# Key searches of four blocks moved from the attention stage into the projection stage, with attention of those blocks first and the weights' upper parts rounded on GpSimd

## The chip, the cores and the metric

The kernel runs on one core of one Trainium2 chip. The metric is the device time of one execution in microseconds (us), the median of three runs.

## The reference

The program computes two layers over one sequence of 2048 positions and width 1024. The change touches the first layer. There, after a root-mean-square norm, one matrix product gives the inputs of two branches. One is a recurrence over the positions (eight heads of 64). The other is sparse attention: each position scores all earlier keys with a small index network, keeps the best 256, and attends to those alone.

```python
def attend(args):                       # one block of 128 queries
    qa, qi, wi, t0 = args
    causal = key_pos[None, :] <= (t0 + jnp.arange(Q_BLOCK))[:, None]
    logits = jnp.einsum('bqhd,bsd->bqhs', qi, k_idx)        # 4 index heads
    score = jnp.einsum('bqh,bqhs->bqs', wi, jax.nn.relu(logits))
    score = jnp.where(causal[None], score, -jnp.inf)
    _, idx = lax.top_k(score, topk)                         # topk = 256
    c_sel = jax.vmap(lambda c, i: c[i])(c_kv, idx)
    s = jnp.einsum('bqhr,bqkr->bhqk', qa, c_sel)            # 8 heads
    s = jnp.where(valid[:, None], s, -jnp.inf)
    return jnp.einsum('bhqk,bqkr->bqhr', jax.nn.softmax(s, axis=-1), c_sel)
```

Both branches are gated, joined, multiplied by an output matrix and added to the input. The second layer is latent attention with rotary positions and a small memory attention; the change leaves it alone.

## The kernel before

**Stages.** The program is a row of stages, each with one function per engine (`pe_a`, `act_a`, `dve_a`, `pool_a` and `sp_a` for the projection stage, the same with `_2` for the attention stage). Between two stages every engine drains and waits for all others.

**Projection stage.** The sequence is taken in four chunks of 512 positions, in two halves of two chunks. The input product has 25 weight tiles of 1024x128. Each is read from memory into `raw_a` (two buffers), rounded to its upper part `wah` (piece `("w", s)`, on ScalarE in `act_a`), and the rest is left in `wal` (VectorE). Both have four buffers. A product of a tile with a chunk (piece `p`) is 24 matmuls: upper by upper, upper by lower and lower by upper, for eight slices. Its results go to one of three PSUM banks and are copied out by ScalarE or VectorE. Beside the products run pieces for the norms and queries (`sum`, `mean`, `qq`), and, for each pair of heads and 256 positions, a chain that makes the operands of the recurrence (`dd`, `lora`, `decay`, `kk`, `vt`, `bk`, `bt`, `bonus`); there are 32 such steps, 16 in each half. `kk` holds a square root, whose table in ScalarE is another than that of exponential and hyperbolic tangent. Input rows are turned and split into `xc` by the pieces `in` and `tr`; the last of them is done soon after the second half has begun, and leaves `xin`, `xtmp` and `xjunk` unused from then on.

**Attention stage.** 16 blocks of 128 queries, the longest first: block `b` has `128 * (nth(b) + 1)` keys, with `nth(b) = 15 - b`. For blocks with more than 256 keys the key search comes first. Piece `log`: matmuls of the index queries with 512 keys, relu on ScalarE, weighted sum on VectorE into `score`, mask on GpSimd. Then the value of the 256th best score is found bit by bit: 31 pieces `bit` on ScalarE (one pass over all keys, Sign of the score against a candidate, with its sum), each followed by `flip` on VectorE (two operations on one column), which makes the next candidate; each waits for the other. `selA` to `selD` settle the threshold, and per 512 keys `eq`, `sel2` and `tie` (GpSimd, VectorE, GpSimd) rank equal scores and write the mask `bias`. Two searches run at a time (lanes `index0`, `index1`).

Attention of a block is four pairs of heads: `score` (matmul, then VectorE adds the mask and takes the maximum), `exp` (ScalarE), `pT` (turn on TensorE, copy by ScalarE or VectorE), `pv` (matmul), `fin`. It waits for the whole mask of its block. Before the first block `kT` and `vv` make keys and values. Beside all this run the 16 steps of the recurrence (`ld` to `yout`).

The order is woven by estimated weights: attention of block `b` beside the second half of the search of block `b + 1` and the first half of that of block `b + 2`:

```python
for t in range(-1, NT + 1):
    parts = [attend_pieces((t - 1,))] if t > 0 else [kv_order] if t < 0 else []
    parts += [index_half(t, True)] if 0 <= t < NT else []
    parts += [index_half(t + 1, False)] if t + 1 < NT else []
    dsa_order += weave(weight, *[x for x in parts if x])
```

**The planner.** `Order.settle` takes the pieces of a stage with the costs written down in `Desk`, keeps the order inside each lane, and always starts the piece that can start first on its engine; of several that can, the one that stands first in the woven list. What comes out is a fixed order per engine, and each engine runs its own strictly in order. SyncE's queue, with all loads and stores, is ordered the same way.

Of the kernel before, what the change touches and what calls it, by code (L numbers as in the profile page):

```python
# [18 lines left out]
NT = T // 128  # L19
# [3 lines left out]
TOPK = 256  # L23
NEG = -3.0e38
# [241 lines left out]
def program(nc, A):  # L266
    ctx = ExitStack()
    with ctx:
# [36 lines left out]
        for name, rows in (("krr", 64), ("qm", 256), ("cos", 128), ("sin", 128)):  # L305
            scratch[name] = nc.dram_tensor("scr_" + name, [rows, T], F32, kind="Internal").ap()
        scratch["mrow"] = nc.dram_tensor("scr_mrow", [48, 4, 128], F32, kind="Internal").ap()
# [87 lines left out]
        bon = SA.sb("bon", [128, UT])  # L395
        SA.c.close()
# [7 lines left out]
        p_pe, p_act, p_dve, p_pool = signal("p_pe"), signal("p_act"), signal("p_dve"), signal("p_pool")  # L404

# [56 lines left out]
        order_a += carry_a  # L462
        order_a = [x for k in order_a for x in ([k, ("xl", k[1])] if k[0] == "tr" else [k])]
# [14 lines left out]
        for k in order_a:  # L478
            who = {"sum": (a_act, "sqrt"), "mean": (a_dve, "mean"), "qq": (a_act, "qq"), "wi": (a_dve, "wi"), "lora": (p_act, "tw1"),
                   "kk": (p_act, "inv"), "bonus": (p_dve, "bonus"), "vt": (p_act, "vt"), "bt": (p_act, "bt")}.get(k[0])  # L480
            if who:
# [5 lines left out]
                small_last[b] = who + k[1:]  # L487
        subs = [(hp, c, s) for half_ in range(2) for hp in range(4) for c in (2 * half_, 2 * half_ + 1) for s in range(2)]
# [15 lines left out]
        def lane_a(k):  # L504
            return {"in": "x in", "tr": "x turned", "xl": "x turned", "w": "w", "p": "p", "th": "th", "dd": "pre0", "lora": "pre0", "decay": "pre0", "kk": "pre1", "bk": "pre1",
                    "vt": "pre2", "bt": "pre2", "bonus": "pre2"}.get(k[0], "sums")
# [3 lines left out]
        def sp_a(q):  # L510
            q.dma(cst[:, :], A["cst"]).then_inc(*d_cst.up())
            for k in q.pieces(turns_a):
# [18 lines left out]
                elif k[0] == "p" and k[1:] in gates_a:  # L531
# [6 lines left out]
                    if (t, c) == (7, 3):  # L538
# [7 lines left out]
                        q.dma(kidx[:, :], scratch["kidx"]).then_inc(*d_kidx.up())  # L546
                elif k[0] in ("bk", "bt", "vt", "bonus"):
# [19 lines left out]
            for e in range(2):  # L567
                q.wait_ge(d_go[e], len(gates_a) - 2 + e)
                q.wait_ge(d_qo[e], len(qqs) - 2 + e)
                q.wait_ge(d_kv[e], 3)  # L570
            q.wait_ge(d_AR, len(subs) - 1)
# [5 lines left out]
        def pe_a(q):  # L577
            q.wait_ge(d_cst)
            for k in q.pieces(turns_a):
                what = k[0]  # L580
                b, empty = small.get(k, (None, None))
# [11 lines left out]
                elif what == "p":  # L593
# [6 lines left out]
                    q.wait_ge(a_act, "wh", s)  # L600
# [61 lines left out]
        def act_a(q):  # L662
# [4 lines left out]
            for k in q.pieces(turns_a):  # L667
                what = k[0]
                if what == "in":
# [118 lines left out]
        def dve_a(q):  # L788
# [6 lines left out]
            for k in q.pieces(turns_a):  # L795
                what = k[0]
                if what == "in":
# [23 lines left out]
                elif what == "w":  # L821
# [3 lines left out]
                    q.wait_ge(a_act, "wh", s)  # L825
# [113 lines left out]
        def pool_a(q):  # L939
# [6 lines left out]
            for k in q.pieces(turns_a):  # L946
                what = k[0]
                if what == "in":
# [5 lines left out]
                         ALU.pow).then_inc(*n_pool.up("rs", i))  # L954
                elif what == "dd":
# [85 lines left out]
        x_pe, x_act, x_dve, x_pool = signal("x_pe"), signal("x_act"), signal("x_dve"), signal("x_pool")  # L1041
        k_act, k_dve, k_pool = signal("k_act"), signal("k_dve"), signal("k_pool")
        t_pe, t_act, t_dve = signal("t_pe"), signal("t_act"), signal("t_dve")
        NR = T // 128

        def weave(weight, *lists):

            marked = []
            for n, x in enumerate(lists):
                at, all_ = 0.0, sum(weight(k) for k in x)  # L1050
                for i, k in enumerate(x):
                    marked.append(((at + 0.5 * weight(k)) / all_, n, i))
                    at += weight(k)
            return [lists[n][i] for _, n, i in sorted(marked)]

        def nth(b):

            return NT - 1 - b

        def chunks(N):  # L1060
            return [(n, 512 * n, min(512, N - 512 * n)) for n in range((N + 511) // 512)]

# [2236 lines left out]
```

## Time and profile before

| | |
|---|---|
| median of 3 runs | 4326.2 us |
| lowest and highest | 4320.02 and 4328.78 us |
| the profiled execution, first to last instruction | 4323.5 us |
| projection stage | 0 to 826 us |
| attention stage | 826 to about 2176 us |
| TensorE busy (matmuls) over the span | 91% |
| VectorE, ScalarE, GpSimd busy | 62%, 49%, 28% |
| mean granted TensorE clock | 0.956 |

The profiled execution lies 2.7 us below the median and between the lowest and the highest run. Busy times are sums of an engine's instructions within a stretch; the granted clock is the share of full speed that TensorE was given. An engine that is busy less than its stretch was waiting, and the rows of waits say for whom.

### The profile page before, as it was taken

To read this page: it belongs to the slowest core of one execution; us is meant where nothing else is said; L and a number is where in the kernel's file an instruction comes from. 1 tells how busy PE (TensorE), PEld (TensorE's weight loads), DVE (VectorE), ACT (ScalarE), POOL (GpSimd) and SP (SyncE) were. 2 spreads that over 40 slices of the span, in tenths; PEclk is the share of its full clock that TensorE was granted. 3 is DMA by queue.
4 is the path that set the end of the run, shared out by engine and by line. 5 is a ranking of instruction groups with operands and counts; after the bars stand their busy time and mean duration, and the time that the engine had idled before them with its cause. 6 is when DMAs were issued, how large, how long until landed. Compare 5 with 4: busy or idle time off the path is not lost. (4 is left out here: it accounts for less than half of the span.)

```text
span 4323.5 us, 76198 instructions
## 1 busy us (share of the span) xinstructions
PE 3949.5 (91%) x31096; PEld 2780.8 (64%) x31096; DVE 2669.1 (62%) x5092; ACT 2122.4 (49%) x3127; POOL 1204.6 (28%) x966
## 2 busy tenths in 40 slices
PE   7989999878988998888789899898999999999889
PEld 5767776546666666666477687686555555555567
DVE  5555555556777787788675323345677777777543
ACT  4444444397777888787443322222333333333431
POOL 1111111125344344434111000000444445454200
PEclk9999999887999999999789999999999999999999
DMA  3334233402111111211255544465232323231243
GB/s 124 95 115 131 83 99 102 124 20 50 34 42 39 47 44 37 56 44 48 86 181 186 197 138 147 167 217 175 52 77 54 80 61 77 55 81 34 99 141 107
DMA packets 388093, 404.95 MB, mean 94 GB/s; under 512 B 115776, under 2 KB 287488, under 8 KB 387488
## 3 DMA queue, kind: packets, MB, share of 16 engines
q1 hardware_dynamic: 386656, 396.77, 31.3%
q8 instruction: 245, 4.01, 0.4%
q10 hardware_dynamic: 1088, 3.32, 0.2%
q14 instruction: 104, 0.85, 0.1%
HBM read 248.36 MB, written 151.62 MB: 93 GB/s over the span
## 5 line engine op out<-in xcount | busy, mean ns | idle before, releaser
L142 ACT ACTIVATE PT<-psum 128x1024 f32<-128x1024 f32 x384 | 394.3, 1027 | 659.6 <-PE psum L132 659.1
L170 DVE TENSOR_REDUCE m<-psum 128x1 f32<-128x1024 f32 x384 | 467.9, 1221 | 274.8 <-PE psum L132 274.8
L132 PE MATMUL psum<-xc,wah 128*128 128x512 f32 x1600 | 514.8, 403 | 3.2 <-DVE xc L146 2.9
L146 POOL TENSOR_TENSOR part<-PT 128x1024 f32<-128x1024 f32 x144 | 341.5, 2371 | 471.4 <-DVE all L146 379.1
L132 PE MATMUL psum<-PT,V 128*64 128x512 f32 x1536 | 371.5, 605 | 0.0
L143 ACT ACTIVATE bias<-score,cand,cols 128x2048 bf16<-128x2048 f32 (+6 forms) x217 | 314.8, 1451 | 85.9 <-DVE cand L153 79.5
L146 POOL TENSOR_TENSOR Lm<-gm,cst 64x512 f32<-64x512 f32 x192 | 257.6, 1342 | 349.9 <-PE psum L132 194.2
L132 PEld LDWEIGHTS psum<-xc,wah 128*128 128x128 f32 x1600 | 300.0, 190 | 79.4 <-issue 10.3
L143 ACT ACTIVATE sgn<-score,cand,cols 128x1920 bf16<-128x1920 f32 (+6 forms) x217 | 291.4, 1343 | 89.5 <-DVE cand L153 84.8
L132 PE MATMUL psum<-hc,w4h 128*128 128x512 f32 x1024 | 320.3, 394 | 8.7 <-DVE w4l L146 8.7
L132 PE MATMUL psum<-xc,wal 128*128 128x512 f32 x800 | 315.9, 395 | 0.0
L132 PEld LDWEIGHTS psum<-hc,w4h 128*128 128x128 f32 x1024 | 193.2, 189 | 52.7 <-issue 12.9
L132 PE MATMUL psum<-m_wh,m_yh 128*128 128x512 f32 x512 | 204.1, 399 | 17.3 <-DVE m_wl L146 17.3
L135 PE MATMUL psum<-cst,P 128*128 128x128 f32 x1088 | 185.6, 299 | 36.3 <-DVE pt L161 18.8
L132 PE MATMUL psum<-kT,qd 64*128 64x512 f32 (+3 forms) x640 | 193.8, 607 | 19.7 <-DVE mx L178 15.3
L132 PEld LDWEIGHTS psum<-PT,V 128*64 128x64 f32 x1536 | 93.3, 136 | 177.9 <-issue 177.6
L178 DVE CUSTOM_DVE_ANT_0 P<-psum,bias 128x512 f32<-128x512 f32 (+3 forms) x320 | 181.9, 605 | 37.9 <-PE psum L132 27.3
L132 PE MATMUL psum<-m_wl,m_yh 128*128 128x512 f32 x512 | 202.3, 395 | 0.0
L132 PE MATMUL psum<-m_wh,m_yl 128*128 128x512 f32 x512 | 202.1, 395 | 0.0
L135 PEld LDWEIGHTS psum<-cst,P 128*128 128x128 f32 x1088 | 122.6, 148 | 122.3 <-issue 45.8
L132 PE MATMUL psum<-hc,w4l 128*128 128x512 f32 x512 | 200.0, 391 | 0.0
L146 DVE TENSOR_TENSOR all<-all,part 128x1024 f32<-128x1024 f32 x144 | 191.5, 1331 | 4.2 <-POOL part L146 4.2
(336 smaller groups left out, 8664.9 us busy)
## 6 DMA issues: line engine op xcount, KB each, us to landing
raw_a<-in_w_a SPq DMA_DIRECT2D x50, 512.0 KB
raw_w<-in_w_in SPq DMA_DIRECT2D x32, 512.0 KB, 5.3
QNh<-scr_qnh SPq DMA_DIRECT2D x48, 256.0 KB, 4.9
QRh<-scr_qrh SPq DMA_DIRECT2D x96, 128.0 KB, 4.6
QNl<-scr_qnl SPq DMA_DIRECT2D x48, 256.0 KB, 6.4
xin<-in_x SPq DMA_DIRECT2D x16, 512.0 KB
scr_AR<-AR SPq DMA_DIRECT2D x32, 256.0 KB, 2.2
scr_BK<-BK SPq DMA_DIRECT2D x32, 256.0 KB, 2.2
```

The costliest lines, as they stand in the source:

```text
L132: return self.e.matmul(out, a, b, start=start, stop=stop, skip_group_check=True)
L135: return self.e.transpose(out, src, ident) if self.e else self.idle(0.17)
L142: return self.e.activation(out, src, f, bias=bias, scale=scale)
L143: return self.e.activation(out, src, f, bias=bias, scale=scale, accum_out=acc)
L146: return self.e.tensor_tensor(out, a, b, op) if self.e else self.vector(out)
L170: return self.e.tensor_reduce(out, a, AX, op, negate=negate) if self.e else self.vector(a)
L178: return self.e.tensor_tensor_reduce(out, a, b, 1.0, -3.0e38, ALU.add, ALU.max, acc)
```

## The change

**Early searches.** A class `Search` holds what one group of searches uses (buffers, signals, what must be free), and the search pieces of each engine are now functions (`index_pe`, `index_act`, `index_dve`, `index_pool`) that both stages call. The first four blocks in a new order, `BLOCKS = (7, 6, 5, 4, 15, ..., 8, 3, 2, 1, 0)`, with 1024, 896, 768 and 640 keys, are the `early` group. Their pieces (`order_e`) are merged into the projection stage's list from the last `tr` on, evenly by count, in two lanes. They use `xin` for scores, `xjunk` and `xtmp[0]` for signs and masks, PSUM banks 4 and 5 for logits (relu in place), and load their keys and queries back from memory. SyncE stores each finished mask.

**Attention stage.** Its queue first loads the four masks. Attention of block 7 (1024 keys) follows keys and values, beside the first half of the search of block 15; attention of 6, 5 and 4 beside that search's second half and the first half of block 14's; then on as before, with block 15.

**Rounding.** The upper parts `wah` of the weights are made by a copy on GpSimd in place of ScalarE. There are 50 of them, 128x1024 each.

The core of the diff:

```diff
+N_EARLY = 4
+BLOCKS = (7, 6, 5, 4, 15, 14, 13, 12, 11, 10, 9, 8, 3, 2, 1, 0)
...
+        early.score = xin
+        early.cols, early.cand, early.flip = ecols, ecand, eflip
+        early.qx, early.d_qx = [eqx], [d_eqx]
+        early.kidx, early.keys_there = [xtmp[1].rearrange("p a b -> p (a b)"), ekidx], (d_eki, 1)
+        signs = [xjunk, xtmp[0].bitcast(BF16).rearrange("p a b -> p (a b)")]
+        early.junk = early.out = lambda b: signs[early.lane(b)]
+        early.relu = lambda k, e: bank[4 + e]
...
+        order_e = []
+        for t in early.blocks + [N_EARLY]:
+            halves_e = ([index_half(t - 1, True)] if t else []) + ([index_half(t, False)] if t < N_EARLY else [])
+            order_e += weave(weight, *halves_e)
...
+        ready = order_a.index(("tr", NT - 1)) + 1
+        order_a = order_a[:ready] + merge(order_a[ready:], order_e)
...
+                elif k[0] == "tie" and k[2] == last_of[k[1]]:
+                    b, n = k[1:]
+                    N = 128 * (nth(b) + 1)
+                    q.wait_ge(early.k_pool, "tie", b, n)
+                    q.dma(scratch["bias"][early.no[b]][:, 0:N], early.out(b)[:, 0:N]).then_inc(*d_ebo[early.lane(b)].up(b))
...
-                elif what == "w":
-                    s = k[1]
-                    q.wait_ge(d_wa[s % 2], s)
-                    if s > 3:
-                        q.wait_ge(a_pe, "p", *last_a[(tiles_a[(s - 4) % NW], (s - 4) // NW)])
-                    q.act(wah[s % 4][:, :, :], raw_a[s % 2][:, :, :], ACT.Copy).then_inc(*a_act.up("wh", s))
...
+                elif what == "w":
+                    s = k[1]
+                    q.wait_ge(d_wa[s % 2], s)
+                    if s > 3:
+                        q.wait_ge(a_pe, "p", *last_a[(tiles_a[(s - 4) % NW], (s - 4) // NW)])
+                    q.copy(wah[s % 4][:, :, :], raw_a[s % 2][:, :, :]).then_inc(*a_pool.up("wh", s))
...
-        for t in range(-1, NT + 1):
-            parts = [attend_pieces((t - 1,))] if t > 0 else [kv_order] if t < 0 else []
-            parts += [index_half(t, True)] if 0 <= t < NT else []
+        first = late.blocks[0]
+        for t in range(first - 1, NT + 1):
+            if t < first:
+                parts = [kv_order + attend_pieces((0,))]
+            elif t == first:
+                parts = [attend_pieces(range(1, first))]
+            else:
+                parts = [attend_pieces((t - 1,))]
+            parts += [index_half(t, True)] if first <= t < NT else []
             parts += [index_half(t + 1, False)] if t + 1 < NT else []
             dsa_order += weave(weight, *[x for x in parts if x])
...
         def sp_2(q):
+            for b in early.blocks:
+                N = 128 * (nth(b) + 1)
+                q.dma(bias_of(b)[:, 0:N], scratch["bias"][early.no[b]][:, 0:N]).then_inc(*d_eb.up(b))
```

## Rows read from the trace of the kernel before

**Rows 1.** The page: TensorE's granted clock in 40 slices of 108 us.

```profile
PEclk9999999887999999999789999999999999999999
```

**Rows 2.** Busy time by stretch: length, each engine (instructions), clock, DMA share, GB/s.

```profile
460.00:800.00 340.00, 329.33 (x1372) 249.23 (x1372) 183.35 (x333) 150.31 (x238) 43.89 (x60) 0.98 0.32 99
800.00:826.00 26.00, 9.36 (x29) 5.53 (x27) 12.77 (x28) 9.10 (x15) 0.86 (x2) 0.60 0.47 165
826.00:920.00 94.00, 86.22 (x957) 48.03 (x957) 61.44 (x112) 65.89 (x89) 33.03 (x24) 0.91 0.27 64
920.00:1034.00 114.00, 69.15 (x1231) 60.62 (x1230) 52.77 (x143) 92.97 (x99) 54.86 (x44) 0.75 0.16 36
1034.00:1100.00 66.00, 57.66 (x798) 38.11 (x798) 47.44 (x122) 50.96 (x63) 28.24 (x22) 0.86 0.14 34
1100.00:2000.00 900.00, 803.28 (x11662) 573.20 (x11658) 709.31 (x2122) 726.75 (x1095) 376.05 (x319) 0.96 0.18 44
2000.00:2176.00 176.00, 128.31 (x1568) 90.42 (x1568) 117.38 (x458) 91.89 (x242) 47.40 (x46) 0.83 0.24 71
```

**Rows 3.** Timeline of ScalarE, two search operations: start, duration.

```profile
929.09 2.01 ACT L143 ACTIVATE sgn<-score,cand,cols 128x1920 bf16<-128x1920 f32 x1
...
931.06 2.11 ACT L143 ACTIVATE bias<-score,cand,cols 128x2048 bf16<-128x2048 f32 x1
```

**Rows 4.** Waits, 830 to 1034 us: total, times, longest.

```profile
PEld psum L132 <- ACT Y L142: 35.3, 11, 10.5
```

**Rows 5.** SyncE's queue: stores of finished blocks (the first, ninth and twelfth).

```profile
1154.77 0.36 SPq L126 DMA_DIRECT2D scr_yT<-gate  x1
...
1830.62 0.36 SPq L126 DMA_DIRECT2D scr_yT<-gate  x1
...
2075.60 0.36 SPq L126 DMA_DIRECT2D scr_yT<-gate  x1
```

**Rows 6.** Timeline of TensorE: projection matmuls, and a pair of logits.

```profile
799.39 0.62 PE L132 MATMUL psum<-xc,wah 128*128 128x512 f32 x2
...
800.08 0.62 PE L132 MATMUL psum<-xc,wah 128*128 128x512 f32 x2
...
840.04 1.04 PE L132 MATMUL psum<-kidx,qx 64*128 64x512 f32 x4
```

**Rows 7.** Groups by shape, ScalarE, 830 to 2173 us: busy us, mean ns.

```profile
L142 ACT ACTIVATE rl<-psum 128x512 f32<-128x512 f32 x112 | 61.4, 587 | 23.2 <-PE psum L132 12.2 <-DVE score L158 6.9 <-DVE score L152 3.9
...
L143 ACT ACTIVATE bias<-score,cand,cols 128x1024 bf16<-128x1024 f32 x31 | 38.2, 1231 | 5.9 <-DVE cand L153 5.8
...
L143 ACT ACTIVATE sgn<-score,cand,cols 128x640 bf16<-128x640 f32 x31 | 28.3, 913 | 10.1 <-DVE cand L153 8.3 <-DVE cand L164 1.5
```

**Rows 8.** The same for VectorE.

```profile
L178 DVE CUSTOM_DVE_ANT_0 P<-psum,bias 128x512 f32<-128x512 f32 x224 | 145.3, 686 | 28.7 <-PE psum L132 21.0 <-POOL bias L153 6.4
...
L153 DVE TENSOR_SCALAR cand<-flip,cand 128x1 int32<-128x1 int32 x434 | 93.0, 214 | 15.4
L153 DVE TENSOR_SCALAR flip<-cols 128x1 int32<-128x1 f32 x434 | 90.3, 208 | 102.9 <-ACT bias L143 54.9 <-ACT sgn L143 44.9
```

**Rows 9.** Groups by shape, ScalarE, 460 to 826 us.

```profile
L142 ACT ACT_TABLE_LOAD x35 | 44.9, 1283 | 0.6
L142 ACT ACTIVATE wah<-raw_a 128x1024 fp32r<-128x1024 f32 x21 | 22.1, 1054 | 12.1 <-PE psum L132 12.1
```

**Rows 10.** SyncE's queue: stores of a recurrence step's operands.

```profile
781.88 0.37 SPq L126 DMA_DIRECT2D scr_AR<-AR  x1
...
806.69 0.37 SPq L126 DMA_DIRECT2D scr_AR<-AR  x1
...
820.47 0.36 SPq L126 DMA_DIRECT2D scr_AR<-AR  x1
```

**Rows 11.** Groups by shape, GpSimd, whole execution.

```profile
L146 POOL TENSOR_TENSOR part<-PT 128x1024 f32<-128x1024 f32 x144 | 341.5, 2371 | 471.4 <-DVE all L146 379.1 <-ACT PT L142 92.3
...
L152 POOL TENSOR_SCALAR rl<-bias 128x512 f32<-128x512 bf16 x16 | 24.1, 1504 | 13.6 <-ACT score L143 12.7
```

More of the change, by code:

```diff
@@ L395, in program @@
         bon = SA.sb("bon", [128, UT])
+        ekidx = SA.sb("ekidx", [128, 512])
+        eqx = SA.sb("eqx", [128, 2, 128])
+        ecols = SA.two("ecols", [128, 10])
+        ecand = SA.two("ecand", [128, 1], I32)
+        eflip = SA.two("eflip", [128, 1], I32)
         SA.c.close()
@@ new lines, in index_pieces @@
+        def index_pieces(b):
+            if nth(b) < TOPK // 128:
+                return [("nobias", b)]
+            ns = [n for n, _, _ in chunks(128 * (nth(b) + 1))]
+            out = [("qx", b)] + [("log", b, n, x) for n in ns for x in range(2)] + [("sel0", b)]
+            for i in range(30, -1, -1):
+                out += [("bit", b, i), ("flip", b, i)]
+            return out + [("selA", b), ("selB", b), ("selC", b), ("selD", b)] + [(x, b, n) for n in ns for x in ("eq", "sel2", "tie")]
@@ new lines, in program, with index_pe @@
+        early, late = Search("e", list(range(N_EARLY))), Search("l", [b for b in range(N_EARLY, NT) if nth(b) >= TOPK // 128])
+        INDEX = ("log", "sel0", "bit", "flip", "selA", "selB", "selC", "selD", "eq", "sel2", "tie")
+        def index_pe(q, I, k):
+            b, n, x = k[1:]
+            w = width(b, n)
+            m = I.no[b] % len(I.qx)
+            q.wait_ge(I.d_qx[m], b)
+            q.wait_ge(*I.keys_there)
+            for e in range(2):
+                o, free = I.ring[k][e]
+                if free:
+                    q.wait_ge(*free)
+                a = 64 * e
+                t = q.mm(o[:, 0:w], I.qx[m][a:a + 64, x, :], I.kidx[n][a:a + 64, 0:w])
+            t.then_inc(*I.x_pe.up("log", b, n, x))
@@ new lines, in program @@
+        early.signals()
+        early.score = xin
[5 more added lines that the diff above has]
+        early.relu = lambda k, e: bank[4 + e]
+        early.ranks = lambda b: [early.score[early.lane(b)][:, 512 * i:512 * i + 512] for i in range(2)]
@@ L570, in sp_a @@
                 q.wait_ge(d_kv[e], 3)
+            for e in range(2):
+                q.wait_ge(d_ebo[e], early.blocks[-2 + e])
             q.wait_ge(d_AR, len(subs) - 1)
@@ L580, in pe_a @@
                 what = k[0]
+                if what == "log":
+                    index_pe(q, early, k)
+                    continue
                 b, empty = small.get(k, (None, None))
@@ L668, in act_a @@
                 what = k[0]
+                if what in INDEX:
+                    index_act(q, early, k)
+                    continue
                 if what == "in":
@@ L796, in dve_a @@
                 what = k[0]
+                if what in INDEX:
+                    index_dve(q, early, k)
+                    continue
                 if what == "in":
@@ L947, in pool_a @@
                 what = k[0]
+                if what in ("log", "eq", "tie"):
+                    index_pool(q, early, k)
+                    continue
                 if what == "in":
@@ L1190, in sp_2 @@
         def sp_2(q):
+            for b in early.blocks:
+                N = 128 * (nth(b) + 1)
+                q.dma(bias_of(b)[:, 0:N], scratch["bias"][early.no[b]][:, 0:N]).then_inc(*d_eb.up(b))
             for k in q.pieces(turns_2):
@@ L1542, in act_2 @@
+                elif what in INDEX:
+                    index_act(q, late, k)
                 elif what == "exp":
@@ L1694, in dve_2 @@
+                elif what in INDEX:
+                    index_dve(q, late, k)
                 elif what == "score":
```

435 lines of the change are left out of this document (241 added, 194 removed).

## The prediction

> **What bounds the kernel now.** I read the page's 40 slices first, for where TensorE is not full, then busy times in stretches cut at the stage borders, then the waits of the weak stretch, then the DMA queue's list of finished blocks, and last the groups by shape, for the prices of what moves.
>
> The slices show a granted clock of 9 tenths nearly everywhere and of 7 in two of them, the tenth (973 to 1081 us) and the twentieth (2054 to 2162) [rows 1]. The stretches say more [rows 2]. The projection stage up to 800 us is TensorE's: 329.33 of the 340 us from 460 on are busy at clock 0.98, while ScalarE has 150.31 and VectorE 183.35. Then 26 us of tail (800 to 826, 9.36 us of TensorE). The attention stage is 826 to about 2176. From 1100 to 2000 TensorE is busy 803.28 of 900 us at 0.96, that is 0.857 us of full-speed work per us; ScalarE is at 81%, VectorE at 79%. From 920 to 1034 it is 69.15 of 114 at 0.75, so 52 us of full-speed work, and from 1034 to 1100 57.66 at 0.86, so 50. ScalarE is busy 92.97 of that 114, mostly with key searches of the two longest blocks, one search operation right behind the other: the next one starts 1.97 us after one of 2.01 [rows 3]. In that hole TensorE's weight loads wait 35.3 us for ScalarE's copies of the recurrence [rows 4]. There is no attention work to give it, since the first attention needs the first search finished: the first finished block is stored at 1154.77, and blocks of 1024 keys and less take the time from 1830.62 to 2075.60, 245 us [rows 5].
>
> **What leaves the attention stage.** The searches of the four blocks with 1024, 896, 768 and 640 keys, their logits and tie passes.
> TensorE: a pair of logit matmuls over 512 keys, four records, takes 1.04 us [rows 6]. The four blocks have 3328 keys, times two head pairs, over 512: 13 pairs, 13 us.
> ScalarE: the 31 operations of a search cost 1.231 us each at 1024 keys and 0.913 at 640 [rows 7]. The four sizes lie evenly, mean 1.072, so 124 of them are 133 us (the reading of the accumulator costs nothing more, as the interval in [rows 3] shows). Five more passes per block are 21 us. The 32 copies of logits are 20 at 0.587 and 12 shorter, 16 us. Together 170 us.
> VectorE: two small operations per bit, 0.214 and 0.208 us [rows 8], 124 times, are 52 us; 32 score operations from PSUM at up to 0.686 us, as the 512-wide row there, are 19; for ranks and the small column operations I put 24, an estimate at two or three times 512-wide operations per chunk. Together 95 us.
> GpSimd: eight chunks of equality and tie, three operations of about 1.5 us each [rows 11], 36 us.
>
> **What the attention stage gains.** The hole gets filled: attention of the four early blocks is ready when keys and values are, about 900, and runs while the two long searches run. I count TensorE work. From 920 to 2000 it is 52 + 50 + 771 = 873 us of full-speed work in 1080 us. 13 leave: 860. At the steady 0.857 this takes 1003 us, 77 less (62 of it the hole, 15 the logits). The steady rate itself should rise a little, since ScalarE falls from 81% (170 us less of some 1030 in 826 to 2176) to some 70%. I take 0.87: 988 us, 92 less. Bounds for the rate are 0.84, about that of 826 to 920 (86.22 at 0.91, over 94), with 57 us less, and 0.90, with 125 less, which every engine would allow. The last 176 us, with attention of the four smallest blocks at clock 0.83, stay as they are; the same pieces end the new order.
> The stage starts with four loads of stored masks on SyncE's queue, ahead of the first recurrence loads. Four issues at some 0.38 us, as the stores in [rows 5], and under a megabyte of transfer: 2 us. Zero if only the keys' path counts there; 5 at most.
>
> **What the projection stage pays.** The logits add 13 us of TensorE, and it has only 11 us idle in 460 to 800, which belong to dependences. So 13 on the path, bounds 2 and 15.
> ScalarE loses 21 roundings of weights of 1.054 us there [rows 9], 22 us, and gains 170: 150 - 22 + 170 = 298 of 340 us, 88%. VectorE goes to 183 + 95 = 278, 82%. Neither is over the length, and results wait in three banks, so a projection's copy may be late by two tiles, some 11 us, before TensorE stops. But the recurrence operands are a chain of both engines. At the tail, with nothing beside it, a sub-step takes 13.8 us (806.69 to 820.47), while inside the stage the steps come every 24.8 us (781.88 to 806.69) [rows 10]. That is 11 us of cover per step; a visit to ScalarE behind one search operation costs up to 1.2 us, seven visits 8.6. The cover holds, with little left. I put 7 us for visits that TensorE feels: it takes the sum, query and operand matmuls strictly in order. Zero to 60 are the bounds.
> Every wait that the searches add has a queue behind it. On ScalarE a bit waits for VectorE's flip, and projection copies stand behind; on SyncE the store of a mask waits for GpSimd's tie, and weight loads stand behind. A tile's 24 matmuls take 5.5 us, three per 0.69 [rows 6]. Weights have four buffers and are refilled about three tiles, 16 us, before use, so these delays of a few us stay hidden. If that cover were gone, each late refill would stop TensorE for its own lateness.
> Rounding on GpSimd: one instruction for 128x1024. The trace has none of this form. A two-input operation of this size takes 2.371 us there, a one-input one over 512 takes 1.504 [rows 11], so 3.0 for 1024; a faster path would be 1.1, as on ScalarE. I take 2.4, nearest in size; 50 of them are 120 us on an engine busy 44 of 340. Hidden in 16 us of slack at either bound; what it costs at the start (VectorE's lower parts later by 1 us in the first 33 us) I put at 0, with bounds of -2 and +3.
> The Trainium skill (GPSIMD Engine Reference, Engine selection) advises VectorE for elementwise work and calls one-input work on GpSimd roughly line-rate. By that the copy would be about 1.1 us, which the row of 1.504 for half the size speaks against; by either, the sum is unchanged.
>
> **Sum.** -92 + 2 + 13 + 7 = -70 us. The profiled execution spans 4323.5 us, 2.7 under the median of 4326.2 and inside the three runs; a difference carries over. 4326.2 - 70 = 4256.
>
> **Rivals.**
> (a) ScalarE and VectorE become the bound of the second half of the projections; this one ends slower. Place: 460 to 826. If each of the seven ScalarE visits of a step waits for an operation of both searches (2.2 us), the step is 13.8 + 15.4 = 29.2 us, 4.4 more than the 24.8 it has; 16 steps are 70 us, with the 13 of logits and the 2 of loads 85. The attention stage then gives only its 77. That is +8 to +15 (VectorE's stalls under GpSimd's copies on top): 4338. It decides from 11 us of delay per step on. For it: 88% and 82%, both in-order. Against: the order lets projection pieces go first when both are ready. Chance 0.14.
> Table loads belong here: 35 of 1.283 us lie in 460 to 826 [rows 9]. There are 22 square roots (16 of operands, 6 of norms), at most 44 loads if searches fall between all of them: 9 more, 12 us of ScalarE, 92% instead of 88%. The Trainium skill (ScalarE: Activation LUTs, Table sets: the hidden batching unit) says that only cheap functions stand in every set and asks to batch by set; its list names no Sign. By that rule loads rise toward the 44; if Sign were in the root's set too, they stay at 35. It moves rival (a)'s chance, not the sum.
> (b) The hole is only half filled. Attention's exponentials and copies queue behind the long searches on ScalarE, which was 82% busy there already; the search of the longest block ends later, and its attention starts late. Gain: 15 for logits and 31 for half of the hole, less 22: 4302. For it: [rows 3, 4]. Chance 0.2.
> (c) The relief of ScalarE and VectorE counts for more, rate 0.90: -125 + 22, 4223. For it: TensorE's idle time in 1100 to 2000 is spread over many waits for both. Against: 0.90 was not held over any long stretch. Chance 0.2.
> (d) No visible change: losses of (a) at half size meet gains of (b). 4320 to 4332. Chance 0.06.
> My forecast, with a range of its own of 4240 to 4280: 0.4.
>
> **How the numbers follow.** The three runs spread over 0.2%, 8.8 us, so less than 0.2% can't be told from no change. The forecast, (b) and (c) are faster, 0.8; (d) is within 0.2%, of which I round the edge up to 0.07; slower is (a) with 0.13. From (c), a little beyond it, to the near edge of (a): 4212 to 4325.
>
> **What the profile would show.** Stored blocks of 1024 keys and less first, the first near 1000 us instead of 1155; clock 0.95 or more in the first 200 us of the attention stage instead of 0.75; ScalarE near 90% from about 465 to 800; last projection matmul at about 820; the tail still near 26 us; attention stage about 1260 us instead of 1350; GpSimd's copies of 2 to 3 us. The prediction is wrong if the steps of [rows 10] come more than 27 us apart, if table loads in the stage pass 44, or if TensorE waits long for weights.

## The result, and the profile after

The changed kernel takes 4220.94 us (median of 4 runs, 4216.89 to 4222.14), beside 4324.94 us for the kernel before on the same chip (4320.02 to 4328.78): a ratio of 0.9756, 95% interval 0.9745 to 0.9768. That is 104 us less. The forecast was 4256, 70 us less. The profiled execution of the changed kernel spans 4218.7 us.

First the stretches, cut where this kernel's own stages end. Columns as in [rows 2].

```profile
460.00:844.00 384.00, 354.39 (x1439) 255.46 (x1440) 278.59 (x662) 289.11 (x521) 100.60 (x103) 0.95 0.29 90
844.00:876.00 32.00, 11.31 (x32) 6.07 (x30) 20.11 (x48) 13.81 (x26) 11.03 (x10) 0.55 0.50 165
876.00:970.00 94.00, 87.44 (x934) 48.59 (x936) 59.02 (x130) 62.77 (x85) 26.98 (x22) 0.95 0.25 59
970.00:1084.00 114.00, 109.55 (x1746) 79.68 (x1742) 88.94 (x260) 98.53 (x129) 36.56 (x34) 0.99 0.23 56
1084.00:1150.00 66.00, 56.16 (x950) 42.89 (x948) 53.16 (x152) 39.33 (x61) 38.86 (x27) 0.97 0.26 66
1150.00:1896.00 746.00, 666.89 (x10387) 485.11 (x10387) 574.11 (x1602) 572.50 (x775) 346.02 (x286) 0.95 0.19 46
1896.00:2072.00 176.00, 148.06 (x2140) 107.34 (x2136) 131.31 (x470) 90.83 (x225) 62.10 (x58) 0.92 0.29 82
```

Two things moved, in opposite directions. The projections end at 844 us instead of 800, and their tail lasts 32 us instead of 26 [rows 2], so the attention stage begins at 876 instead of 826: 50 us lost. The attention stage then takes 1193 us (876 to 2069) instead of 1347 (826 to 2173): 154 us won. The stretch that held the hole, 920 to 1034 before with 69.15 us of TensorE in 114 at clock 0.75, answers to 970 to 1084 here: 109.55 of 114 at 0.99, with ScalarE at 98.53 us (92.97 before).

SyncE's queue, the stores of finished blocks (those of [rows 5]), shows what fills it.

```profile
989.73 0.62 SPq L128 DMA_DIRECT2D scr_yT<-gate  x1
...
1060.56 0.36 SPq L128 DMA_DIRECT2D scr_yT<-gate  x1
...
1103.74 0.36 SPq L128 DMA_DIRECT2D scr_yT<-gate  x1
...
1142.18 0.36 SPq L128 DMA_DIRECT2D scr_yT<-gate  x1
```

The four blocks of 1024 to 640 keys are done 266 us after the stage begins. Before, no block at all was done until 1154.77, and these four took 245 us near the end of the stage.

The same queue, stores of a recurrence step's operands, as in [rows 10]; ten more lie between the first two shown.

```profile
485.69 0.38 SPq L128 DMA_DIRECT2D scr_AR<-AR  x1
...
792.10 0.38 SPq L128 DMA_DIRECT2D scr_AR<-AR  x1
...
815.34 0.37 SPq L128 DMA_DIRECT2D scr_AR<-AR  x1
...
839.05 0.37 SPq L128 DMA_DIRECT2D scr_AR<-AR  x1
...
856.28 0.37 SPq L128 DMA_DIRECT2D scr_AR<-AR  x1
...
870.02 0.37 SPq L128 DMA_DIRECT2D scr_AR<-AR  x1
```

From 485.69 to 839.05 there are 13 steps of 27.2 us each. The same 13 took 23.2 us each before (480.13 to 781.88). Groups by shape say what runs beside them, for ScalarE from 460 to 844 us and for GpSimd from 33 to 850.

```profile
L144 ACT ACT_TABLE_LOAD x30 | 38.5, 1283 | 0.5
L145 ACT ACTIVATE xjunk<-xin,ecand,ecols 128x1024 bf16<-128x1024 f32 x31 | 38.3, 1235 | 4.3 <-DVE ecand L155 4.3
L145 ACT ACTIVATE xtmp<-xin,ecand,ecols 128x896 bf16<-128x896 f32 x31 | 34.9, 1126 | 8.5 <-DVE ecand L155 8.4
L145 ACT ACTIVATE xjunk<-xin,ecand,ecols 128x768 bf16<-128x768 f32 x31 | 31.7, 1022 | 9.1 <-DVE ecand L155 9.0
L145 ACT ACTIVATE xtmp<-xin,ecand,ecols 128x640 bf16<-128x640 f32 x31 | 28.5, 918 | 14.3 <-DVE ecand L155 14.1
```
```profile
L163 POOL CAST wah<-raw_a 128x1024 fp32r<-128x1024 f32 x46 | 52.1, 1132 | 204.1 <-PE psum L134 196.9 <-DMA raw_a<-in_w_a 7.0
```

The passes cost what they cost before (133.4 us together). The rounding is one instruction of 1.13 us on GpSimd, not 2.4. ScalarE is busy 75% of the stretch (289.11 of 384) and VectorE 73%: neither is full, and yet the steps are 4 us longer. Up to 800 us alone it is the same, 255.28 us of ScalarE in 340. What TensorE meets there is seen best between 674 and 682 us. This is the timeline, ScalarE's passes and the square that TensorE waits for.

```profile
674.96 0.83 ACT L145 ACTIVATE xjunk<-xin 128x768 bf16<-128x768 f32 x1
...
675.78 1.12 ACT L145 ACTIVATE xtmp<-xin,ecand,ecols 128x896 bf16<-128x896 f32 x1
...
677.38 1.02 ACT L145 ACTIVATE xjunk<-xin,ecand,ecols 128x768 bf16<-128x768 f32 x1
...
678.38 1.12 ACT L145 ACTIVATE xtmp<-xin,ecand,ecols 128x896 bf16<-128x896 f32 x1
...
679.50 1.02 ACT L145 ACTIVATE xjunk<-xin,ecand,ecols 128x768 bf16<-128x768 f32 x1
...
680.51 1.04 ACT L144 ACTIVATE sq<-raw 128x1024 f32<-128x1024 f32 x1
...
681.70 1.19 PE L134 MATMUL psum<-sq,cst 128*128 128x512 f32 x1 [5.47 <-ACT sq L144]
```

Five passes of two searches, with one copy of 0.58 us between them (676.90), stand ahead of the norm's square in ScalarE's order, and TensorE is idle for 5.47 us until the square is there. All its waits from 460 to 844 us add up to 29.3 us: 18.2 end with ScalarE and 11.1 with VectorE (7.7 and 2.8 before, from 460 to 800). The clock falls there too:

```profile
650.00:700.00 50.00, 32.59 (x90) 15.62 (x89) 39.71 (x86) 40.41 (x71) 4.61 (x7) 0.77 0.31 94
700.00:750.00 50.00, 48.18 (x175) 31.04 (x174) 38.88 (x92) 41.21 (x77) 15.64 (x14) 0.93 0.39 118
```

### The profile page after: what moved, and what is told of

It is laid out like the page before. It is cut to its first block and busy times, and to the rows that moved or that the text cites. A ratio compares the mean times of both kernels' runs of the same rounds, so it can differ in the third digit from the quotient of the medians.

```text
span 4218.7 us, 76240 instructions
## 1 busy us (share of the span) xinstructions
PE 3902.4 (93%) x31096; PEld 2741.9 (65%) x31096; DVE 2696.0 (64%) x5092; ACT 2076.1 (49%) x3079; POOL 1278.6 (30%) x1016
## 5 line engine op out<-in xcount | busy, mean ns | idle before, releaser
L145 ACT ACTIVATE bias<-score,cand,cols 128x2048 bf16<-128x2048 f32 (+4 forms) x155 | 244.5, 1577 | 76.2 <-DVE cand L155 72.3
L145 ACT ACTIVATE sgn<-score,cand,cols 128x1920 bf16<-128x1920 f32 (+4 forms) x155 | 227.9, 1470 | 60.3 <-DVE cand L155 58.8
L180 DVE CUSTOM_DVE_ANT_0 P<-psum,bias 128x512 f32<-128x512 f32 (+3 forms) x320 | 181.8, 605 | 26.1 <-PE psum L134 23.2
L148 POOL TENSOR_TENSOR all<-PT 128x1024 f32<-128x1024 f32 x48 | 114.6, 2388 | 272.3 <-ACT PT L144 272.3
```

The source lines that it names most:

```text
L145: return self.e.activation(out, src, f, bias=bias, scale=scale, accum_out=acc)
L148: return self.e.tensor_tensor(out, a, b, op) if self.e else self.vector(out)
L180: return self.e.tensor_tensor_reduce(out, a, b, 1.0, -3.0e38, ALU.add, ALU.max, acc)
```

## Experiments

Twelve kernels ran, in three rounds of four. In each round the kernel before ran on the same chip (medians 4320.98, 4324.22 and 4325.98 us), and each ratio is to it. Where two changed kernels are compared below, the difference is that of their medians, and under some 5 us it says little. The part of the kernel behind the attention stage, which no experiment touches, differs by up to 10 us between their profiled executions (2151.7 us from the last stored block to the end in experiment 10, 2161.3 in experiment 7).

**1. The new order of blocks with no search of the early ones.** The four early blocks get the causal mask alone, so their searches are left out altogether.

```diff
-            order_e += weave(weight, *halves_e)
+            order_e += []
...
+                parts = [kv_order + attend_pieces((0,)), [("nobias", x) for x in early.blocks]]
```

> The changed kernel without the four early searches: blocks of 1024 to 640 keys attend under the causal mask alone, so the output differs. Everything else as changed. Theory 1 (the searches cost the projection stage what its last matmul moved, 800.5 to 843.5 us, and a longer tail, 50 us in all): 4221 - 50 = 4171 us, last projection matmul near 800, attention stage 1193 us as in the changed kernel. Rival (rounding on GpSimd or the changed list costs part of the 50): last projection matmul still at 815 or later, 4185 to 4200.

Measured: 4177.56 us (4174.23 to 4180.12), ratio 0.9662 (0.9643 to 0.9681), 43 us under the changed kernel. Its windows:

```profile
460.00:798.00 338.00, 326.40 (x1370) 248.61 (x1371) 185.06 (x327) 129.15 (x214) 70.65 (x79) 0.99 0.32 99
829.00:2027.00 1198.00, 1079.77 (x16144) 772.74 (x16143) 904.53 (x2610) 861.38 (x1270) 514.57 (x432) 0.95 0.21 53
```

The last projection matmul is back at 798 us, while the attention stage (828 to 2024, 1196 us) is as long as with the early searches (1193). So the whole price of searching early is paid in the projection stage: 43 us.

**2. The old order, with no search of the same four blocks.**

```diff
-            if nth(b) < TOPK // 128:
+            if nth(b) < TOPK // 128 or 4 <= nth(b) < 8:
                 return [("nobias", b)]
...
```

> The kernel before, order of blocks unchanged, without the searches of the blocks of 1024 to 640 keys (causal mask alone, the output differs). Splits the attention stage's gain of 154 us into order and relief. If the hole at the start is what was gained (as forecast: 62 of 77), this gives only the logits and some relief late in the stage: 20 to 40 us, 4285 to 4305. If the relief of ScalarE and VectorE in the second half of the stage is the larger part: 80 us or more, under 4245.

Measured: 4235.79 us (4234.51 to 4240.69), ratio 0.9802 (0.9785 to 0.9818): 85 us less, where the prediction gave 30 (15 for logits, 15 for a better rate). The stores of the blocks concerned, 245 us apart before [rows 5], are now 169 us apart. The first line is the kernel before, from the first stored block to the eighth, the second its next four blocks; the other two are the same in this kernel.

```profile
1154.80:1830.60 675.80, 602.16 (x8674) 426.47 (x8674) 531.45 (x1553) 549.23 (x777) 283.13 (x235) 0.96 0.18 45
1830.60:2075.60 245.00, 210.22 (x3306) 155.34 (x3302) 200.10 (x680) 192.13 (x408) 102.29 (x93) 0.96 0.18 47
```
```profile
1150.50:1821.70 671.20, 611.21 (x9560) 448.44 (x9556) 513.36 (x1458) 485.26 (x666) 307.27 (x259) 0.96 0.20 49
1821.70:1990.60 168.90, 156.17 (x2454) 115.89 (x2452) 129.79 (x437) 92.00 (x207) 52.85 (x49) 1.00 0.19 50
```

The stores alone mislead. Some 850 matmuls have left the last stretch (2454 records for 3306), and about as many more are done between the first block and the eighth (9560 for 8674) in nearly the same time. So part of the 85 us was won beside the longer blocks, as other work done earlier.

**3. The order alone: the old kernel with blocks 7 to 4 first, every search in the attention stage.**

```diff
-            return NT - 1 - b
+            return (7, 6, 5, 4, 15, 14, 13, 12, 11, 10, 9, 8, 3, 2, 1, 0)[b]
```

> The kernel before with only the order of blocks changed (1024, 896, 768, 640 keys first), all searches in the attention stage, projections untouched. The first search is half as long as that of 2048 keys, so attention can start some 50 us earlier, but the long searches then fall beside short attentions. Theory hole: 30 to 70 us less, 4255 to 4295. Theory relief: no gain, since ScalarE has the same work in the stage: 4315 to 4345.

Measured: 4334.53 us (4330.16 to 4340.34), ratio 1.0028 (1.0018 to 1.0038), 14 us slower. The first block is stored at 1027.33 us, the fourth only at 1278.05. Window of 920 to 1034, beside [rows 2]:

```profile
920.00:1034.00 114.00, 83.69 (x1338) 63.62 (x1340) 77.25 (x237) 86.40 (x155) 49.12 (x42) 0.84 0.13 31
```

The hole is filled by about a third (83.69 us of TensorE after 69.15, where the changed kernel has 109.55), and the stage is 14 us longer all the same. With experiments 1 and 2 this makes a square: while the four searches are in the stage, the order costs 14 us; once they are out, it gives 58 (4235.79 to 4177.56). The second pair differs in more than the order, since experiment 1 has the rounding on GpSimd as well; experiment 5 puts that at nothing in the old kernel. The square is made of the order and the absence of the searches; the old order with the searches moved early was not run.

**4. The changed kernel with the rounding back on ScalarE.**

```diff
+                    q.act(wah[s % 4][:, :, :], raw_a[s % 2][:, :, :], ACT.Copy).then_inc(*a_act.up("wh", s))
...
-                    q.copy(wah[s % 4][:, :, :], raw_a[s % 2][:, :, :]).then_inc(*a_pool.up("wh", s))
```

> The changed kernel with the rounding of the weights back on ScalarE, 50 operations of 1.054 us, 21 of them beside the searches. Theory that ScalarE's order and load set the pace of the projection stage in its second half: 22 us of ScalarE added to some 330 of 384, 5 to 20 us slower than the changed kernel, 4226 to 4241. Theory that VectorE or TensorE sets it: within 4 us of 4221.

Measured: 4237.49 us (4222.14 to 4240.88), ratio 0.9797 (0.9773 to 0.982): some 16 us slower than the changed kernel, with one of its runs level with it. Its profiled execution is 19 us longer, but its masks are loaded only 5 us later (881.62 us); the rest comes in the attention stage and behind it, where the two kernels are alike, and is not explained.

**5. The old kernel with the rounding alone on GpSimd** (the diff of 4, the other way round).

> The kernel before with only the rounding of the weights' upper parts moved from ScalarE (1.05 us each) to GpSimd (1.13 us each in the changed kernel). Theory A: ScalarE does not bound the projections while no search runs beside them, so the time stays between 4314 and 4323 us. Theory B: the rounding was also in the way before (the kernel with the change and the rounding left on ScalarE was some 16 us slower), then 4305 to 4312 us.

Measured: 4327.42 us (4322.76 to 4333.11), ratio 1.0006 (0.9997 to 1.0016). No change: theory A (just above its 4314 to 4323, level with the kernel before). ScalarE falls from 150 to 130 us in 460 to 800, and TensorE's busy time stays (328.33 us, 329.33 before):

```profile
460.00:800.00 340.00, 328.33 (x1377) 249.21 (x1378) 185.48 (x329) 129.78 (x216) 70.71 (x79) 0.99 0.33 101
```

The small edit of the change is worth nothing by itself. Beside the searches it is worth 5 us of the projection stage, and what it has to do with the other 11 is open.

**6. Ties go to the projections.** The planner goes through the pieces in time and, of those that could start together, takes the one listed first; here all search pieces are listed last.

```diff
-        order_a = order_a[:ready] + merge(order_a[ready:], order_e)
+        order_a = order_a + order_e
```

> The changed kernel with the search pieces listed behind all projection pieces, so that the planner prefers a projection piece whenever both could start at the same planned moment. Theory C (ties in the planner's order cost the 43 us by which the projections end later): 4180 to 4205 us, last projection matmul before 825 us. Theory D (the load of ScalarE costs them): 4217 to 4226 us, last projection matmul 840 to 847 us.

Measured: 4381.48 us (4378.01 to 4387.53), ratio 1.0137 (1.0122 to 1.0152). Slower than both kernels, and neither theory's number. The last projection matmul is at 802 us, but the stored masks are loaded, ahead of the first recurrence loads, at 1029.88:

```profile
1029.88 1.74 SPq L128 DMA_DIRECT2D bias<-scr_bias  x4
```

The logits, without which no search can begin, went behind: 12 of their 64 matmuls run before the projections end (from 642 us on), the other 52 after. TensorE has a projection piece ready at nearly every moment, so they probably lost their ties there; this is argued, not shown. The searches then ran by themselves after the projections, 154 us beyond the 876 us of the changed kernel. That accounts for the 160 us between the two.

**7. Short passes.** The order is that of the changed kernel; the 124 passes look at 128 columns.

```diff
-                q.act(j, s, ACT.Sign, bias=f, scale=cv[:, 0:1], acc=cv[:, 5:6]).then_inc(*I.k_act.up("bit", b, i))
+                m = 128 if q.e and I is early else N
+                q.act(j[:, 0:m], s[:, 0:m], ACT.Sign, bias=f, scale=cv[:, 0:1], acc=cv[:, 5:6]).then_inc(*I.k_act.up("bit", b, i))
...
```

> The changed kernel with the same order of instructions, but the 124 passes over the bits in the projection stage look at 128 columns instead of 640 to 1024 (an estimate of 0.5 us each instead of 1.08, so 71 us less of ScalarE); which keys are kept is no longer right. Theory D (ScalarE's load sets the pace): the projections end 30 to 43 us earlier, 4180 to 4192 us. Theory E (the extra matmuls of the logits, the chains of small steps on VectorE and the fixed order cost the time): 4205 to 4220 us.

Measured: 4212.15 us (4210.72 to 4215.76), ratio 0.9746 (0.973 to 0.9762), 9 us less than the changed kernel. (In the profiled executions the last block is stored 18 us earlier, at 2047.80 after 2066.15, and the part behind it is 9 us longer.) The passes of one of the two buffers, in the groups by shape:

```profile
L145 ACT ACTIVATE xjunk<-xin,ecand,ecols 128x128 bf16<-128x128 f32 x62 | 30.3, 489 | 22.8 <-DVE ecand L155 22.5
```

A pass takes 489 ns, so 73 us of ScalarE are gone (133.4 less 60.6), and the last projection matmul comes at 829 us, 15 earlier. The window up to there:

```profile
460.00:829.00 369.00, 347.67 (x1429) 253.03 (x1428) 271.76 (x655) 217.99 (x516) 97.80 (x101) 0.97 0.30 94
```

With ScalarE at 59%, the projections still end 31 us later than with no search. Theory D gave 30 to 43 us for this, so the length of the passes does not set the pace by itself; the total is theory E's. But load is not ruled out: ScalarE still has 89 us more than with no search (217.99 after 129.15), 61 of them the passes' own 489 ns. Taking 71 of the added 160 us off ScalarE (289.11 less 217.99) took off 15 of the 46 us.

**8. Short passes in the old kernel**, for the same four blocks in their old place.

> The kernel before, but the 124 passes over the bits of blocks 7 to 4 look at 128 columns instead of 640 to 1024, in the old place and order (the kept keys of these blocks are no longer right). Leaving out the whole searches of these blocks in this order was worth 85 us of the total. Theory F (what the searches cost the attention stage is ScalarE's time): 66 us less work on ScalarE give at least two thirds of that, 4250 to 4270 us. Theory G (it is the number of small steps and their chains, and the logits on TensorE): 4290 to 4315 us.

Measured: 4313.23 us (4306.56 to 4322.46), ratio 0.9971 (0.9961 to 0.998): 13 us, where leaving the searches out gives 85. Theory F falls: the passes take 60.4 us instead of 133.0, and these 73 of ScalarE's 163 us for the four searches (1028.46 in the attention stage before, 864.99 in experiment 2) give about a seventh of the 85, not two thirds. The 60 us of short passes stay in, and what they cost is not shown.

**9. Search pieces yield on every engine**: the planner takes one only if no projection piece can start there within 2 us.

```diff
-                        if own is None or (go, place[k]) < own[:2]:
+                        rank = go + (self.late if name.startswith("index") else 0.0)
+                        if own is None or (rank, place[k]) < own[4:]:
```

> The changed kernel with the planner told to take a search piece on an engine only if no projection piece can start there within 2 us. Theory C (projection pieces standing behind search passes in ScalarE's order cost the 43 us): last projection matmul before 830 us and 4185 to 4210 us. Theory D (load): the searches only end later, 4215 to 4235 us.

Measured: 4387.29 us (4381.29 to 4390.9), ratio 1.0147 (1.0132 to 1.0162). It repeats experiment 6: last projection matmul at 796 us, masks loaded at 1034.59.

**10. They yield on ScalarE and VectorE only**, within 1 us; TensorE takes the logits as before.

```diff
+                        rank = go + (self.late if e in ("act", "dve") and name.startswith("index") else 0.0)
```

> The changed kernel with the planner told to take a search piece on ScalarE and VectorE only if no projection piece can start there within 1 us; TensorE keeps its order by the same plan, so the logits still run early. Theory C (projection pieces behind search passes in the fixed orders of ScalarE and VectorE cost most of the 43 us): last projection matmul at 800 to 822 us, though the searches end later and the attention stage can begin only after them, so the total may be anywhere from 4200 to 4270 us. Theory H (the work itself costs it: matmuls, table loads, small steps): last projection matmul at 832 us or later.

Measured: 4272.56 us (4267.17 to 4274.33), ratio 0.9879 (0.9864 to 0.9893). Its windows, and its longest wait of TensorE from 820 to 920 us (total, times, longest):

```profile
460.00:811.00 351.00, 341.12 (x1417) 252.00 (x1418) 237.90 (x523) 229.49 (x391) 88.94 (x94) 0.98 0.32 99
811.00:918.00 107.00, 13.51 (x47) 7.80 (x45) 51.68 (x182) 75.14 (x152) 15.63 (x17) 0.54 0.15 49
918.00:2117.00 1199.00, 1069.32 (x16144) 764.74 (x16144) 906.00 (x2610) 861.70 (x1269) 509.82 (x425) 0.95 0.21 54
```
```profile
PE psum L134 <- SPq L189: 78.4, 1, 78.4
```

The last projection matmul is at 811 us, 32 earlier than in the changed kernel, as theory C had it (the total lies just past its 4270). But the last two searches end later and the attention stage can only begin at 918 (876 in the changed kernel): TensorE waits 78.4 us there. And this is not the order alone. Only 69 of the 124 passes are done before the last projection matmul, and ScalarE is busy 229.49 us up to there, where the changed kernel has 289.11. The cleanest comparison ends at 650 us. From 460 on, the changed kernel has done 52 passes by then, with TensorE busy 179.62 of 190 us at 0.97; this one has done 39, with TensorE busy 189.53 at 0.99. With a quarter fewer passes, TensorE is idle for 0.5 us instead of 10.4. That speaks for the order, but does not measure it.

**11. Short logit matmuls**, 64 columns wide, in the changed kernel's order.

```diff
-                t = q.mm(o[:, 0:w], I.qx[m][a:a + 64, x, :], I.kidx[n][a:a + 64, 0:w])
+                m_ = 64 if q.e and I is early else w
+                t = q.mm(o[:, 0:m_], I.qx[m][a:a + 64, x, :], I.kidx[n][a:a + 64, 0:m_])
```

> The changed kernel in the same order, but the 64 matmuls of the logits in the projection stage are 64 columns wide instead of 128 to 512 (their scores are no longer right): about 13 us less of TensorE. If TensorE's time is what the projections pay for, the last projection matmul comes 8 to 13 us earlier and the total is 4208 to 4214 us; if the chains through ScalarE and VectorE set the pace, 0 to 3 us earlier and 4218 to 4223 us.

Measured: 4221.21 us (4216.39 to 4228.25), ratio 0.9763 (0.9749 to 0.9778). The projections end 8 us earlier, at 836 us, but the total is that of the changed kernel.

```profile
460.00:836.00 376.00, 346.92 (x1431) 254.96 (x1432) 275.62 (x656) 285.94 (x515) 97.91 (x101) 0.94 0.30 92
```

In the profiled executions the last block is stored 3.6 us earlier (2062.60 after 2066.15), so half of the 8 us went in the attention stage, which is the same in both; the spread of the runs is 12 us.

**12. Short passes and short logits together.**

> Short passes (worth 9 us of the total and 15 us at the last projection matmul when alone) and short logit matmuls together, in the changed kernel's order. If the two costs are separate parts of the 43 us, the last projection matmul is at 815 to 820 us and the total 4196 to 4204 us; what is then left against 798 us is the number of small steps and their fixed order. If it stays near 828 us, the chains are all that is left.

Measured: 4209.33 us (4205.13 to 4219.7), ratio 0.9738 (0.9723 to 0.9753). Last projection matmul at 829 us, as with short passes alone.

```profile
460.00:829.00 369.00, 346.47 (x1432) 256.30 (x1433) 275.88 (x658) 218.53 (x519) 99.03 (x101) 0.94 0.30 94
```

The two parts don't add up, and the lines of the stretches say where the second went. Idle time is a stretch less its busy time, the clock takes the busy time times what is missing to 1, and the rest is full-speed work. The clock has two digits and each kernel one trace, so a figure can be off by 2 us.

| from 460 us to the last projection matmul | idle | taken by the clock | full-speed work |
|---|---|---|---|
| no search (1) | 12 | 3 | 323 |
| changed kernel | 30 | 18 | 337 |
| short passes (7) | 21 | 10 | 337 |
| short logits (11) | 29 | 21 | 326 |
| both (12) | 23 | 21 | 326 |

The short logits do save 11 us of work, alone and with the short passes. But with both, the granted clock is 0.94 where short passes alone have 0.97, and that takes the 11 us back. The stretch from 650 to 700 us is where they differ most: TensorE is busy 34.22 us of 50 at 0.69 in this kernel, and 33.74 at 0.83 in experiment 7. Why the clock differs for nearly the same busy time is not shown. What still holds the 31 us of lateness is open between the places of the pieces in the fixed orders, the chains of small steps, VectorE's 91 us of added work, which no experiment took away by itself, and ScalarE's own 89.

Of the kernels that compute everything (3 to 6, 9 and 10), none beats the changed one.

## Why the prediction was right, and where its sizes were not

The total falls inside the range (4212 to 4325) and the direction is right. But it is 35 us off the forecast, and two terms were mis-sized in opposite directions; that their errors partly cancel, 55 us against 23, is luck. The amounts of work that leave the attention stage were sized well: between the kernel before and experiment 2 it is 163 us of ScalarE (170 predicted), 85 of VectorE (95) and 25 of GpSimd (36). What they are worth was not. By terms of the sum, from the experiments:

- **The filled hole, 62 us predicted: held.** 58 us by experiments 1 and 2, and only with the searches out of the stage; with them in it the same order costs 14 (experiment 3). The clock of the first 200 us of the stage is 0.95 to 0.99, the first block is stored at 990 us, and the masks' loads take 1.8 us (876.21 to 878.01), with 2 predicted.
- **The relief of the stage, 30 us predicted: mis-sized, 85 measured.** This is the step "the steady rate itself should rise a little ... I take 0.87". The direction was right, the rise much larger: between the first stored block and the eighth, experiment 2 does 14.2 matmuls per us, the kernel before 12.8. By the prediction's measure, busy time times clock, it is 0.874 after 0.855, which looks like the small rise that was forecast. And it took the last 176 us as fixed, though 76 of the 245 us of these blocks lie in them. The measure misled as well. These are the attention stages of the kernel before and of experiment 2.

```profile
826.00:2176.00 1350.00, 1144.63 (x16208) 810.37 (x16208) 988.33 (x2955) 1028.46 (x1583) 539.58 (x453) 0.92 0.19 48
```
```profile
827.00:2087.00 1260.00, 1088.95 (x16144) 785.58 (x16144) 903.06 (x2611) 864.99 (x1272) 514.54 (x432) 0.93 0.20 51
```

The matmuls fall by 64, those of the logits, 13 us of work, yet TensorE's busy time falls by 56 us at nearly the same clock. Busy time times clock thus holds waiting that goes away with the searches. In the changed kernel it gives 0.849 for 1150 to 1896 us, below the 0.857 of before, while the matmuls per us rise from 12.96 (11662 in 900) to 13.92 (10387 in 746), though the mix of shapes is not the same. Rival (c) had this mechanism, and its 4223 came within 2 us of the result, but by luck: as 125 won and 22 paid, where the runs show 143 won and 43 paid.

- **What of the searches costs the stage those 85 us** is only partly settled. Shorter passes on ScalarE give 13 back (experiment 8). Between before and experiment 2 VectorE has 85 us less to do and TensorE 13 us of logits; these, and the chains, were not taken apart.
- **The projections, 20 us predicted: mis-sized, 43 measured** (experiment 1), with 50 at the start of the attention stage. The 13 us of logits are there: full-speed work of TensorE up to the last projection matmul is 337 us (354.39 at 0.95) against 323 (326.40 at 0.99), 14 more in 46 more. The step that failed is "I put 7 us for visits that TensorE feels": it was some 30. By the table of experiment 12, the rest of the 46 us is 18 of idle time (30 after 12) and 14 of lower clock (18 after 3), for which the prediction put nothing in this stage. The sign of being wrong that the prediction set itself, steps over 27 us apart, came at 27.2. It was set beside 24.8 us, a single interval; the 13 steps before had a mean of 23.2.
- **Rival (a)** happened in its place and nearly in its size: a step cost 4.0 us more where the rival had 4.4. Passes of both searches ahead of a visit are seen too. Its load was not reached: ScalarE was at 75%, not 88%, and VectorE at 73%, not 82%. How far ScalarE alone was the cause is open; taking 73 us of work off it gave 15 back, and 11.1 of TensorE's 29.3 us of waits end with VectorE. What the rival's total missed is that the attention stage won 154 us, not 77.
- **"The order lets projection pieces go first when both are ready"**, said against rival (a), was wrong. The order is fixed in advance from planned times; on the chip five passes stood ahead of the square that TensorE waited 5.47 us for. In experiment 10, where they yield, and in experiment 1, where there are none, its longest wait for a square is 1.7 us.
- **The tail, 26 us predicted, is 32.** The last mask is stored at 860.23 and the last operands at 870.02, so the searches reach into it.
- **Of the other signs**, the first stored block (989.73 us, near 1000 forecast) and the clock of the hole came as forecast. ScalarE is at 75% from 460 to 800 us, not near 90; the last projection matmul is at 844 us, not 820; the attention stage takes 1193 us, not 1260.
- **GpSimd's copy, 2.4 us predicted, took 1.13.** By the Trainium skill (GPSIMD Engine Reference, Engine selection) one-input work there is roughly line-rate. The trace agrees for this form, at 1.13 us beside 1.054 on ScalarE [rows 9]; the nearest row by size was the wrong one to take. The total didn't hang on it.
- **Table loads did not rise.** ScalarE has 34 of them from 440 to 876 us, and 36 from 440 to 850 before, with 124 more operations that compute a sign among the square roots. The bound of 44 was not approached (the 92% beside it should be 91). By the Trainium skill (ScalarE: Activation LUTs, Table sets: the hidden batching unit) loads come when the set changes. That sign passes between roots brought none fits their being in the root's set too, though its list doesn't name them.

## What to carry to other kernels

Moving work under another stage and reordering what depended on it can be worth far more together than the sum of both. Here the order alone lost 14 us, taking the searches out alone won 85, and both won 143, of which 43 were paid where the searches went. Run both halves and the pair before judging either.

In a statically ordered program, the idle share of a stage is not its cover. With ScalarE at 75% and VectorE at 73%, TensorE stood idle for 18 us more and lost 14 more to a lower clock. Look at what stands ahead of each instruction on the path, and split a lost stretch into idle time, clock and work before asking for its cause.

Don't count work by busy time when the engine waits in small pieces: two stages with the same matmuls but 64 differed by 56 us. Compare stretches that hold the same instructions.

## What the runs showed of the hardware

A GpSimd copy from f32 to fp32r of 128x1024 took 1.13 us, less than the one-operand operation from bf16 to f32 on half as many columns (1.50 us) and half of the two-operand one of its own size (2.37 us) [rows 11]. On ScalarE a pass with an accumulated sum over 128 columns takes 489 ns and one over 1024 columns 1235, so some 382 ns of it do not shrink with the width ((1235 - 489) / 896 = 0.833 ns a column; at 640 columns this line gives 915, and 918 were measured). By that line, an estimate, a search's 31 passes cost some 12 us of ScalarE however few its keys.

The granted clock was lowest where TensorE stood idle most. In the changed kernel it was 1.00 from 500 to 600 us, with TensorE busy 98.99 of 100 us, and 0.77 from 650 to 700, with 32.59 of 50. Beside the 18 us of added idle time up to 844 us, the lower clock cost 14 more. Busy time alone does not settle it: at 33.74 and 34.22 us of 50 the clock was 0.83 and 0.69 (experiments 7 and 12).
